# Expert weights in one piece per partition, issued in the order their buffers come free, and VectorE's slot numbers moved behind gate halves

## What is computed

```python
expert_id = g_idx[:, None] * EXPERTS_PER_GROUP + top_i          # 2 of 16 per token
combine = sum(one_hot(expert_id, N_EXPERTS) * (g_w * top_w)[..., None], axis=1)
hid = silu(einsum('td,edf->tef', xt, w_gate)) * einsum('td,edf->tef', xt, w_up)
out = einsum('tef,efd->td', hid * combine[..., None], w_down)   # D_MODEL 1024, D_EXPERT 512
```

## Time and profile before

| | |
|---|---|
| median of 3 runs | 835.08 us (833.68 to 836.03) |
| profiled execution | 832.79 us, span 831.1 us |
| busy, share of the span | PE 719.1 us (87%), DVE 531.9 (64%), ACT 407.1 (49%), POOL 167.1 (20%) |
| DMA | 183.75 MB, mean 221 GB/s |
| load queue (q1) | 58080 packets, 161.39 MB |
| GpSimd's queue (q0) | 7312 packets, 19.61 MB |

### The profile page before, as it was taken

The page is one execution under the profiler, slowest core; times in us unless marked ns, Lnnn a source line. Parts: engine busy times, 40 slices in busy tenths (PEclk is TensorE's granted clock), DMA queues, the critical chain, the costliest instruction groups (busy, mean ns, idle before and its releaser), DMA issues. The chain is left out here.

```text
span 831.1 us, 10457 instructions
## 1 busy us (share of the span) xinstructions
PE 719.1 (87%) x3772; PEld 544.2 (65%) x3772; DVE 531.9 (64%) x799; ACT 407.1 (49%) x602; POOL 167.1 (20%) x168
## 2 busy tenths in 40 slices
PE   2898999899999989999985389999999989999800
PEld 1248998849898755555544368877777777778600
DVE  5345526367512057565435669999988999999648
ACT  1454533411223144555322357777777677777433
POOL 2000000000022047542210302333333333331000
PEclk9999999999999989999987589999999999999955
DMA  9993115211398191000008983999999999999163
GB/s 325 407 400 114 58 45 203 101 43 73 128 179 320 65 394 44 1 26 2 26 26 274 396 303 106 372 377 365 352 362 362 355 357 347 360 363 361 55 269 128
DMA packets 67196, 183.75 MB, mean 221 GB/s; under 512 B 4592, under 2 KB 4624, under 8 KB 63824
## 3 DMA queue, kind: packets, MB, share of 16 engines
q1 hardware_dynamic: 58080, 161.39, 52.2%
q0 software_dynamic: 7312, 19.61, 6.8%
q10 hardware_dynamic: 1760, 2.17, 0.8%
HBM read 175.26 MB, written 14.19 MB: 228 GB/s over the span
## 5 line engine op out<-in xcount | busy, mean ns | idle before, releaser
L1407 DVE TENSOR_TENSOR WL<-slot,WH 128x1024 fp32r<-128x1024 f32 x192 | 222.0, 1218 | 1.3 <-ACT WH L970 1.0
L970 ACT CAST WH<-slot 128x1024 fp32r<-128x1024 f32 x192 | 187.1, 1052 | 25.5 <-DMA slot<-in_w_up 16.0
L1606 PE MATMUL bank<-WH,xgTh 128*128 128x512 f32 x256 | 103.7, 405 | 17.8 <-DVE WL L1407 16.4
L1606 PE MATMUL bank<-hTh,WP 128*128 128x384 f32 (+1 forms) x320 | 99.6, 311 | 2.2 <-DVE hT L1123 2.2
L1606 PE MATMUL bank<-WL,xgTh 128*128 128x512 f32 x256 | 101.0, 394 | 0.0
L1606 PE MATMUL bank<-WH,xgTl 128*128 128x512 f32 x256 | 100.9, 394 | 0.0
L1606 PE MATMUL bank<-hTl,WP 128*128 128x384 f32 (+1 forms) x320 | 99.4, 311 | 0.0
L1606 PE MATMUL bank<-hTh,WL 128*128 128x384 f32 (+1 forms) x320 | 99.4, 311 | 0.0
L1510 PE MATMUL bank<-slot,big 128*128 128x512 f32 (+1 forms) x224 | 91.7, 559 | 1.6 <-issue 1.6
L705 POOL DMA_INDIRECT y_scratch<-big x16 | 67.1, 4196 | 108.5 <-DVE big L1440 108.5
L1519 PE MATMUL bank<-ident,big 128*128 128x128 f32 x424 | 62.2, 287 | 14.0 <-DMA big<-h_scratch,big 8.2
(11 more groups left out here) (226 smaller groups left out, 1081.4 us busy)
## 6 DMA issues: line engine op xcount, KB each, us to landing
slot<-in_w_gate SPq DMA_DIRECT2D x16, 2048.0 KB, 14.0
slot<-in_w_up SPq DMA_DIRECT2D x16, 2048.0 KB
slot<-in_w_down SPq DMA_DIRECT2D x16, 2048.0 KB, 9.2
slot<-in_w_ada SPq DMA_DIRECT2D x12, 2048.0 KB, 13.1
slot<-in_w_in SPq DMA_DIRECT2D x6, 2048.0 KB, 17.4
big<-in_x SPq DMA_DIRECT2D x2, 2560.0 KB, 20.4
big<-y_scratch SPq DMA_DIRECT2D x5, 1024.0 KB, 8.9
big<-m_scratch POOLq DMA_DIRECT2D x8, 512.0 KB, 9.1
```

Of the source, the lines that this page charges most:

```text
L970: act.copy(WH[:, high_half(w, s), r, :], quarter(s, w, r)).then_inc(high_ok[w], 1)
L1407: dve.tensor_tensor(WL[ESLOT[3 * s + w]][:, r, :], quarter(s, w, r), WH[:, high_half(w, s), r, :].bitcast(F32), ALU.subtract).then_inc(low ...
L1606: ins = pe.matmul(out, l[u], r[v], start=first and i == 0, stop=last and i == 2)
```

## The change

Three things. (1) The host lays the weights out anew, so that what a partition gets in one load is one run of 16 KB in memory: before, a load of gate, up, `w_in` or `w_out` had 8 pieces of 2 KB for each partition, down 4 of 4 KB, `w_ada` 2 of 8 KB. The bytes, and the place of each in SBUF, are the same. (2) SyncE issues gate and up of expert e + 1 ahead of down of expert e. (3) VectorE takes `rows_low` and two quarters of gate ahead of `keep_rows` and `numbers`, the other two quarters behind them.

```diff
-                return a["w_ada"][c[2] * 2 * P:(c[2] + 1) * 2 * P, c[1] * AW:(c[1] + 1) * AW].rearrange("(k p) n -> p k n", p=P)
-            w = {"win": a["w_in"], "wout": a["w_out"]}[c[0]]
-            return w[:, c[1] * 512:(c[1] + 1) * 512].rearrange("(k p) n -> p k n", p=P)
+                return a["w_ada"][c[1], c[2]]
+            return {"win": a["w_in"], "wout": a["w_out"]}[c[0]][c[1]]
...
+            def load_weights(j, e, s, ended=None):
+
+                if ended is not None:
+                    sp.wait_ge(used[j], ended * 4)
+                w = (wg, wu, wd)[j]
+                src = w[bass.ds(e, 1), :, :] if not isinstance(e, int) else w[e:e + 1, :, :]
+                sp.dma_start(slot[ESLOT[3 * s + j]], src.rearrange("a p n -> p (a n)")).then_inc(ew_in[3 * s + j], 16)
...
-            load_expert(1, 1)
-            with sp.Fori(1, pairs) as i:
-                for s in range(2):
-                    load_expert(i * 2 + s, s, i * 2 + (s - 1))
+            for j in range(3):
+                load_weights(j, 1, 1)
+
+            def ahead(e, s):
+
+                for j in range(2):
+                    load_weights(j, e, s, e - 1)
+            ahead(2, 0)
+            with sp.Fori(1, pairs - 1) as i:
+                ahead(i * 2 + 1, 1)
+                load_weights(2, i * 2, 0, i * 2 - 1)
+                ahead(i * 2 + 2, 0)
+                load_weights(2, i * 2 + 1, 1, i * 2)
+            ahead(NE - 1, 1)
+            for e in (NE - 2, NE - 1):
+                load_weights(2, e, e % 2, e - 1)
...
+                following = m is None or m + 1 < NE
+                if following:
+                    rows_low(n + 1)
+                    low_parts(0, n + 1, 1 - s, range(2))
                 if m != NE:
                     keep_rows(n, s)
                 if more:
                     dve.wait_ge(sidx_ok, n + 1)
                     numbers(n + 2, s)
-                if m is None or m + 1 < NE:
-                    rows_low(n + 1)
-                    low_parts(0, n + 1, 1 - s)
+                if following:
+                    low_parts(0, n + 1, 1 - s, range(2, 4))
...
+    def rows(w, cuts, parts):
+
+        n = w.shape[-1] // cuts
+        v = w.reshape(*w.shape[:-2], parts, -1, P, cuts, n)
+        return np.moveaxis(v, (-2, -5, -3, -4), (-5, -4, -3, -2)).reshape(*w.shape[:-2], cuts, parts, P, -1)
```

More of the change, by code:

```diff
@@ L539, in load_chunk @@
                         full(sp, *LAST_JOB[before[-1]])
[L540 to L543, removed]
+                sp.dma_start(slot[IN_SLOT[i]], chunk_src(CHUNKS[i])).then_inc(chunk_in[IN_SLOT[i]], 16)
             load_chunk(0)
@@ L557, in _, with load_expert @@
             wg, wu, wd = a["w_gate"], a["w_up"], a["w_down"]
[L559 to L570, removed]
+            def load_weights(j, e, s, ended=None):
[4 more added lines that the diff above has]
+                sp.dma_start(slot[ESLOT[3 * s + j]], src.rearrange("a p n -> p (a n)")).then_inc(ew_in[3 * s + j], 16)
+            def load_expert(e, s, ended):
+                for j in range(3):
+                    load_weights(j, e, s, ended)
             full(sp, *LAST_JOB[-1])
-            load_expert(0, 0, rest=lambda: full(sp, "rt", NT - 1))
+            for j in range(2):
+                load_weights(j, 0, 0)
+            full(sp, "rt", NT - 1)
+            load_weights(2, 0, 0)
             sp.wait_ge(h2_out[0], 16 * 3)
             sp.wait_ge(h2_out[1], 16 * 2)
-            load_expert(1, 1)
-            with sp.Fori(1, pairs) as i:
-                for s in range(2):
-                    load_expert(i * 2 + s, s, i * 2 + (s - 1))
+            for j in range(3):
+                load_weights(j, 1, 1)
+            def ahead(e, s):
+                for j in range(2):
+                    load_weights(j, e, s, e - 1)
[8 more added lines that the diff above has]
+                load_weights(2, e, e % 2, e - 1)
             sp.wait_ge(route_ok, 1)
@@ L1401, in rows_low, with low_parts @@
                        .then_inc(xl_ok, 1)
-            def low_parts(w, n, s):
-                for r in range(4):
+            def low_parts(w, n, s, quarters=range(4)):
+                for r in quarters:
                     dve.wait_ge(high_ok[w], n * 4 + (r + 1))
@@ L1973 @@
         "ck": g["cache_k"][0, 0].reshape(CTX, CH), "cv": g["cache_v"][0, 0].reshape(CTX, CH),
-        "w_ada": g["w_ada"][0], "b_ada": quads(g["b_ada"][0].reshape(ADA_GROUPS, 4, 512)), "w_in": g["w_in"][0],
-        "w_out": g["w_out"][0], "w_gate": g["w_gate"][0], "w_up": g["w_up"][0], "w_down": g["w_down"][0],
+        "w_ada": rows(g["w_ada"][0], ADA_GROUPS, ADA_PARTS), "b_ada": quads(g["b_ada"][0].reshape(ADA_GROUPS, 4, 512)), "w_in": rows(g["w_in"][0], 6, 1)[:, 0],
+        "w_out": rows(g["w_out"][0], 2, 1)[:, 0], "w_gate": rows(g["w_gate"][0], 1, 1)[:, 0, 0], "w_up": rows(g["w_up"][0], 1, 1)[:, 0, 0], "w_down": rows(g["w_down"][0], 1, 1)[:, 0, 0],
         "g1c": cols(g["norm1_g"][0]), "g2r": quads(g["norm2_g"][0].reshape(1, 2, 512))[0], "fg": g["final_g"],
```

2 lines of the change are left out of this document (removed).

## The result

The changed kernel takes 828.97 us (median of 11 runs, 823.41 to 834.66); the kernel before took 833.92 us in the same comparison (11 runs, 831.39 to 836.69). The ratio is 0.9939, with a 95% interval of 0.9912 to 0.9966. The forecast was a gain of 13 us; the gain is 5. The profiled execution took 830.01 us, with a span of 828.3 us.

A forecast was written before the change was run, and what follows sets the result against it. The prediction took the loop through VectorE's wait for the scatter (19.4 us a step) as the bound. Span 831.1 - 15.0 (loop) - 0.5 (front) + 2.5 (first gather) = 818.1 us, hence a median of 822 us, range 816 to 833.

The forecast's parts named there:

- the 15.0: Expert loop: twelve steps of 18.1 us, 217.2 us against 232.2, a gain of 15.0 us (bounds 17.4 and 11.4).
- The sign named as decisive: Landing of the scatter in the expert loop: 12 to 13.5 us means the forecast case, above 15 the slower one.
- the cover of the gather: Expert loop: gather at worst 5.3 us later against 5.5 us between its landing and the turning of its rows, so hidden.
- The price of the pieces: GpSimd's gathers and scatters beside 16 KB load pieces: 1 to 2 us later landing expected in the loop.
- The bound of 4.3 us: A gather or scatter wholly beside loads: 8.3 packets per engine, each 0.52 us longer, lands 4.3 us later.
- The first gather: Start of the experts, where nothing hides the later landing: +2.5 us, bounds 0 and 4.3.
- The term of -0.5 us for the front: Front's modulation weights in 16 KB pieces, waited for by TensorE's weight loads: -0.5 us, bounds -1.9 and +0.5.
- VectorE's order: Expert loop: takes 3.5 us from the loop through the scatter, 19.4 to 15.9 us, so it no longer binds.
- The issue order: SyncE's expert loads leave at three places of a step: worth nothing by itself, but needed for a step of 18.1 us.
- The scatter binds in part: Rival, expert loop: a scatter 3 us later makes the step 18.9 us; about 832 us (826 to 834), chance 0.18.
- the scatter takes the place of the wait: Rival, expert loop: scatter takes 15.8 us beside queued loads, loop 20.2 us; 849 us, slower, chance 0.12.
- Memory is the bound: Rival, expert loads: reads cannot exceed 355 GB/s, so a step stays 19.4 us; 837 us, chance 0.05.

## Why the prediction was wrong

The time lies inside the range (816 to 833) and on the side that had 0.80, but that is luck: the gain was 5 us, not 13, and it came about otherwise than in the sum. The loop gave 6.6 us of the 15.0, and the beginning lost more. The orders were worth 2.5 us more than the sum had them (17.5), the expert pieces took 10.9 of that, and the upper part of the range had been left open for a wait on the scatter, not on the gather. The sign named as decisive, a scatter that lands after 12 to 13.5 us, came true (12.65) and decided nothing.

**The step that failed** is the cover of the gather: "1.0 + 4.3 = 5.3 us at worst, against 5.5. Both are hidden, the scatter narrowly." The 5.5 us were read from the old step, 13.2 us from the gather's start to its turning less 7.7 us. But the edit itself shortens this time. The slot numbers, and the gather behind them, stand 3.5 us further back in VectorE's work, and only the stall of about 1.4 us that goes (19.35 - 17.9) is given back: 2.1 us less. The trace of the kernel with both orders and small pieces shows it: from 585.48, where the gather starts, to 596.53, where its rows are turned, are 11.05 us, and with a mean landing of 8.0 the cover is 3.0 us, not 5.5 less 1.0. Over the loop the time from start to turning is 10.2 to 11.7 us. (Nor did the gather instruction take 1.0 us more: in the loop it takes 1.12 to 1.47 us, and only the last one 1.93.) I had used the 3.5 us to relieve the scatter's loop and forgotten that they are taken from the gather. By the same sum, 8.0 + 4.3 = 12.3 us would have stood against 11.05: a wait of 1.3 us. The largest waits of the changed kernel are 2.1 and 2.2.

**The price of the pieces** was the second error. The gather's mean landing is 2.8 us later than with small pieces (10.8 against 8.0), the scatter's 4.1 (12.65 against 8.5). So the value I chose, "1 to 2 us", was too small. It rested on the expectation that the transfers would often fall between two loads; with small pieces no microsecond of the loop falls below 200 GB/s, and in the changed kernel the load queue is dry mainly behind TensorE's stalls. The bound of 4.3 us for a transfer wholly beside loads was about right for the gather: its longest landing, 12.7, is 4.7 later. It was a little low because a gather or scatter of the loop has 144 packets, 9 for each engine; the 133 of the earlier trace rows are those that fall in its two microseconds. By 9 x 0.52 the bound is 4.7 us. For the scatter it did not hold, as told below. The exchange of packets one for one holds as far as this: with both orders and expert pieces of up to 4 KB, GpSimd's queue moves hardly more packets than the load queue in any microsecond of the loop that the two fill (at most 1.2 for one). With 16 KB pieces such a microsecond may look like this (581 to 582 us of the changed kernel), 26 packets beside 25:

```profile
q1 hardware_dynamic: 26, 0.43, 99.3%
q0 software_dynamic: 25, 0.03, 8.1%
```

Against 105 and 83 in the earlier trace rows, a packet of GpSimd's queue comes up three to four times less often. Other microseconds differ: from 596 to 597 us, where the load queue has 0.27 of the engines' time, it is 16 beside 139. The Trainium skill ("DMA: Bandwidth & Descriptors", Queues, rings and completion order) says that a DMA engine changes between its queues after a whole packet of typically 9 to 17 descriptors. If the packets of the trace were such descriptors, the counts would not have to keep near one for one within a microsecond; here they do at 2, 8 and 16 KB in the microseconds shown, and no run here tells how the two kinds of packet relate.

That the pieces are a condition for a step of 18.1 us was wrong too. With small expert pieces the DMA's share is 1.03 and the step 17.89 us, and larger pieces do not move more in the loop (384, 386, 388 and 369 GB/s), though single loads stood at 406 and 440 in the earlier trace rows.

**The scatter's delay** goes to twice the gather's: up to 7.5 us over the 8.5. The two stand close together now (589.95 and 592.90 us in the step above, 6.4 us apart before) in one queue, so the scatter has the gather's packets ahead of it. The steps fit: gathers of 12.6 and 12.7 us are followed by scatters of 16.0 and 15.1, gathers of 8.9 and 9.5 by scatters of 9.6 and 8.3. Where the two start 5.2 us apart (the slot numbers earlier), scatters of 15.0 us follow gathers of 4.6, but with the instruction of 5.26 us; that is 3.4 over the 11.6 of the kernel before, one transfer's delay and not two. This reading was not tested by a kernel of its own.

**The first gather** was put at +2.5 us (bounds 0 and 4.3). It is 12.59 us of waiting against 7.78 with small expert pieces: +4.8, and +4.3 against the earlier trace rows. A part of it came back because everything ahead of the first gather ran 2.3 us earlier in this profiled execution. That is no effect of the packing: the first gather starts between 462.3 and 466.4 us in the kernels with the front packed and between 462.7 and 465.3 in those without, and the unpacked front, measured above, costs nothing. The term of -0.5 us for the front is therefore 0 within what can be measured.

**The clock** was left out of the sum. In the kernel with small pieces it is granted in full over the 200 us (1.00); in the changed one 0.98. Between 530 and 730 us two stalls of over 2 us are each followed by 1.6 us more of TensorE's work, as read above. With the waits of 6.6 us that makes 9.8 of the 10.9 us by which its twelve steps are longer (225.6 against 214.7). It also cost something at the start: behind the wait of 12.59 us TensorE is still at the lower level from 480 to 484 us (0.50), where the kernel before has the full clock (1.00), and it takes 17.2 us to the next turning (475.04 to 492.20) against 15.9 (472.96 to 488.88). That is most of what the first turning's 2.1 us grow to by 527.41, 3.3 us.

**VectorE's order** was right in direction and too small. That it opens the scatter's loop, and that TensorE and VectorE then bind at about 17.9 to 18.1 us, held: the step is 17.89 us with small pieces, TensorE never idle, VectorE busy 197 of 200. The twelve steps gave 17.5 us there, the best bound of 17.4. The spare time of the scatter was larger than my 2.2 us, because its landing fell to 8.5 us: GpSimd's instruction for it took 1.85 us, not 5.25.

**The issue order** was called worth nothing by itself, but a condition. The condition is shown: without it ScalarE waits 43 us in twelve steps, VectorE 12.9 us for ScalarE, and the step is 19.0 us. "Nothing" was too kind, since alone it costs 0.8%; the cause of that stays open.

**The rivals.** "The scatter binds in part" (832 us) and "the scatter takes the place of the wait" (849 us) both had the right resource, the delay of GpSimd's queue, at the wrong place: TensorE's wait for the gather comes first, and the scatter shows in 4.5 us of VectorE's waits. Where the slot numbers are put decides which of the two it is. Before all four gate quarters it is the scatter (844 us), after them the gather (836), in the middle a little of both (829): with 16 KB pieces none of the three places hides both, with pieces of up to 8 KB the place of the change does. "Memory is the bound" is out, at 384 GB/s over 200 us.

What stays open in part is why the landings of one and the same kernel vary by 4 us (gather) and 8 us (scatter) from step to step. That they do so with 16 KB pieces and hardly with 4 KB (7.7 to 8.6 and 8.3 to 9.3) is measured. A part of it is in the stalls themselves: behind each of the three longest waits of the changed kernel (turnings at 602.66, 660.43 and 699.26 us) the load queue runs dry, as at 610 us above, and the next gather lands after 9.5, 10.0 and 8.9 us. So a late gather makes room for the next one, and the waits do not follow in every step. How the packets meet the loads in the other steps was not taken apart.

## What to carry to other kernels

In this kernel a larger piece for loads that already fill the queue gave nothing and made the gathers and scatters on the same DMA engines wait by the piece. So price small gathers and scatters at their packets per engine times the time of one piece, and take the upper end when the load queue is to be kept full. When work is moved past an instruction to open one loop, recompute the slack of everything behind that instruction in the new step; slack read from the old step is no longer there. And measure the parts of a combined change apart as well as together: here two orders of -0.3% and +0.8% were worth 2.1% as a pair, and the third part took most of it back; 4 KB pieces with both orders (814.6 us) or the old layout (815.2) beat both kernels.

## What the runs showed of the hardware

GpSimd's scatter instruction has two durations. It took 5.25 us in the loop of the kernel before and 1.85 us in the changed one (the row at 592.90 above), while VectorE's work beside it was the same: the scatter starts 0.26 us after the first of four weight parts in a row. With 5.25 us it ends about 0.9 us after the fourth part has ended, with 1.85 about as long after the first. In the loop of both kernels and of all ten experiments the pause of GpSimd ahead of it separates the two: 4.1 or 5.4 us of pause went with 5.25 us, 0.3 and 1.8 us of pause with 1.74 to 1.97, with one exception (the issue order alone, at 693.26 us: 5.4 us of pause and 1.85 us). I had expected 1.85 us for the kernel with the later slot numbers from this, and it took 1.74 to 1.97. The Trainium skill ("SBUF — State Buffer", SBUF: two separate sides) describes a port pair that VectorE and GpSimd share as a lock, held for a whole instruction, with the other engine fully blocked; a VectorE instruction with two SBUF inputs, such as a weight part (`slot` minus `WH`), contends for it only with a GpSimd instruction that reads SBUF. The ends just behind a VectorE instruction would agree with that if the scatter's instruction reads SBUF, which the trace does not say; why GpSimd gets in after the first part in one case and after the fourth in the other, the page does not say either, and no run here separates. In the landing it is worth about 3 us: 8.8 us with VectorE's order alone against 11.6 before, in the same layout.

The second is how sharply the time answers: 8 KB pieces delay the gather by 2.2 us and cost nothing that is clear of noise (0.3%, the intervals overlap), 16 KB pieces delay it by 2.8 and cost 1.5%. The difference is in the longest landings (10.8 against 12.7 us, with 11.1 us to the turning), not in the mean.
